# A two-block transformer on one core: which modulation rows are made where, which chunk load goes first, and how the first expert queries are formed

## The chip, the cores and the metric

One core of a Trainium2 chip runs the whole program. The metric is device time in microseconds of one execution. A core has TensorE (PE, matmuls and transposes), VectorE (DVE), ScalarE (ACT), GpSimd (POOL) and SyncE (SP); in this kernel SP only issues transfers, and POOL mostly issues gathers. Sixteen DMA engines serve the queues of all of them.

## The reference, cut to what matters

Everything is f32, with 256 tokens of 1024 columns. `x` passes the first block (two layers), then the second (two layers), in which 256 context tokens run along.

```python
for l in range(2):                                   # first block
    h = layer_norm(a*h + 0.5*swiglu(h, ffn1...))     # 2816 hidden
    h = layer_norm(a*h + mix(h @ w_in) @ w_out)      # conv, recurrence, pool
    h = layer_norm(a*h + cross_attn(h, mem, ...))
    h = layer_norm(a*h + 0.5*swiglu(h, ffn2...))
for i in range(2):                                   # second block
    mod  = silu(c)     @ ada_w[i] + ada_b[i]         # 6 x 1024 columns
    modc = silu(c_ctx) @ ada_w[i] + ada_b[i]
    h  = modulate(rms_norm(x,  gain1), sh1, sc1)     # h*(1+scale)+shift
    hc = modulate(rms_norm(xc, gain1), csh1, csc1)
    x = x + g1 * (attention(h, hc) @ w_o[i])
    if i == 0: xc = xc + cg1 * (attention(hc, hc) @ w_o[i])
    h2 = modulate(rms_norm(x, gain2), sh2, sc2)
    x = x + g2 * peer_ffn(h2)
    if i == 0: xc = xc + cg2 * peer_ffn(modulate(rms_norm(xc, gain2), ...))
```

`peer_ffn` makes 8 queries of 256 columns for each token, takes the best 16 of 128 x 128 expert keys for each, fetches for each of those 128 experts a row of `u` and a row of `v`, and adds `gate * gelu(u . h2) * v`.

## The kernel before

**Stages.** The context tokens of the second block's first layer come first (0 to about 237 us): the first modulation columns, qkv, `ctx_attention` in four units of four heads and queries, then W_o and the keys of their experts. Then the first block runs for x (to about 1763 us). Its feed forwards take the hidden columns in FT = 22 tiles: on PE `gate_up(ft)` (L1494, 32 matmuls) and `down(ft)` (L1502, 16), on DVE `hidden_tile(ft)`, which multiplies silu(gate) by up. `gate_up` runs a tile ahead, so the order at the end of one is gate_up(21), down(20), down(21). Beside it POOL gathers the experts of the context tokens (L697, 512 KB each) and DVE takes their dot products and weighted sums in `some_slots`. After the last layer_norm the second block does x: qkv, attention, W_o, `first_scores` (the first queries and keys), and then 256 gathers of pairs a layer (L738, 1 MB each) with their products, and the same for the second layer.

**The chunk ring.** Weights other than those of the feed forwards come over one SP queue in chunks of 512 KB into `wring`, four slots; `chunk_done` counts consumed chunks, and a load waits for the chunk four before it. SP works strictly in order, so a load that waits holds all behind it. `ff_loads` fill the feed forwards' own places `fw` on the same queue, three transfers a tile, two tiles ahead. `query_loads` and `kept_load` fetch query weights of the second block into places that are free by then.

**The modulation rows.** silu(c) and silu(c_ctx) times `ada_w` is made in rows of 512 output columns, each from four chunks (2 MB). 12 rows go through the ring. A row is made in one of two ways:

- on PE, `mod_row_part` (L839): two matmuls of 2 rows x 512 columns a chunk, in one of the gaps that `ctx_attention` or a layer_norm has; ACT's `mod_row_take` copies the row out and stores it
- on DVE, `mod_row_sums` (L3092 once and L3095 seven times): the chunks are scaled and added into `row_acc`, `chunk_done` gets all four counts after the last, then one PE product (L1526) sums over partitions.

Rows 0 and 1 are made by PE inside `ctx_attention`, row 2 in the context's `peer_scores`. Each of the two layers of the first block makes four: one on DVE at the end of each feed forward (before `hidden_tile(21)`, with L1526 just before `down(21)`), and one on PE in each of two layer_norms (after cross attention and after the second feed forward). `ROW_AT` says which columns a row holds. At the start of the second block all rows have been stored and are read back into `mod_tm`; PE transposes them, and DVE adds the bias into `mods` and `gains`.

**The tail of the context tokens.** `finish` (L1451) transposes their summed experts in 16 transposes, and a gated add (L2598, eight operations) puts them into `ctx_t`; both stand in `first_scores(0)` now, far from where the context tokens' second-layer keys are made.

**The first queries.** After W_o's last group, x is squared (ACT), averaged over columns by PE (L806), the root is taken on ACT, inverted on DVE (L2380), multiplied into x (L2383), and ACT `modulate` scales and shifts each of eight column groups. `first_queries` (L1218) then waits for `mod_ready(k)` for each and multiplies; ACT takes the result, `part_scores` (L1227) compares it with the keys, and DVE's `first_head` finds the indices for which POOL's first gather waits. In the second layer `own_query` (L902), the attention part left over, stands before and after them, four products each.

Of the kernel before, what the change touches and what calls it, by code (L numbers as in the profile page):

```python
# [21 lines left out]
ALU = mybir.AluOpType  # L22
# [34 lines left out]
CTX_MOD_ROWS = 3  # L57
ROW_AT = 0, 1, 2, 4, 3, 5, 6, 7, 8, 9, 10, 11
# [14 lines left out]
ROW_LOADS = (FIRST_ADA - WR + QKV_CHUNKS + WO_CHUNKS + 2 * PQ_CHUNKS) // WR + CTX_MOD_ROWS + 1  # L73

# [133 lines left out]
def program(nc, a, out):  # L208

    with ExitStack() as ctx:  # L210
# [67 lines left out]
        ada_in = sems(" ".join(f"ada_in_{s}" for s in range(GR)))  # L278
        ff_done = [gate_done, up_done, down_done]
# [74 lines left out]
        def vec(tile, where, name, i=0, n=1):  # L354
# [51 lines left out]
        pq_b = view(arena, 4096, 16, P)  # L406
        probs_b = view(arena, 4096, 2, 2 * T)
# [26 lines left out]
            ctx_t.rearrange("p k t -> p (k t)")[:, i * D:(i + 1) * D] for i in range(2)] + [  # L434
            view(arena, at, D) for at in (14848, 15872, 13824)]
# [56 lines left out]
        def _(eng):  # L492
# [55 lines left out]
            for l in range(L):  # L548
                mix_at, row_at = l * MIX_CHUNKS, CTX_MOD_ROWS + 4 * l
                for w in range(2):  # L550
# [3 lines left out]
                    if w == 0:  # L554
                        mod_row_loads(row_at)
                    else:
                        chunk_loads(a["mix_w"], mix_at + (MIX_CHUNKS - WR), WR)
                        mod_row_loads(row_at + 1)
                        mod_row_loads(row_at + 2)
                    with sp.loop(FT_TURNS, **ff_turn) as i:  # L560
                        for ft in range(FT_STEP):
                            for part in range(3):
                                ff_loads(i * FT_STEP + (l * (2 * FT) + (w * FT + 2 + ft)), ft, part)
                    if w == 0:
                        chunk_loads(a["mix_w"], mix_at, MIX_CHUNKS - WR)
                    else:
                        mod_row_loads(row_at + 3)
# [51 lines left out]
            load(0, a["second_w"][FIRST_ADA + QKV_CHUNKS + WR])  # L619
            for i, dead in enumerate(KEPT_DEAD[DEAD_EARLY:]):  # L620
                load(1 + i, a["second_w"][FIRST_ADA + QKV_CHUNKS + WR + 1 + i])
                kept_load(0, FIRST_ADA, dead)
# [122 lines left out]
        def _(eng):  # L745
# [329 lines left out]
            def block_attention():  # L1075
# [3 lines left out]
                tm_group(2, ps_b[:, 512:D], h2)  # L1079
                qk_stats(0, 4, True)  # L1080
# [47 lines left out]
            def ctx_weighted(u):  # L1128
# [7 lines left out]
                if u < 2:  # L1136
                    mod_row_free()
                else:
# [7 lines left out]
            def ctx_attention():  # L1146
# [16 lines left out]
            def first_scores(l):  # L1163

                rms(FIRST_BLOCK)
                if l == 1:
                    for k in range(4):
                        own_query(1, k, ps_a[:, 1536:2048], LAST_BLOCK)
                if l == 0:
                    finish()  # L1170
                    eng.wait_ge(mod_tm_in, 16)
                    nc.tensor.transpose(ps_d[:, 0:2 * ADA_CHUNKS], mod_tm[0:2 * ADA_CHUNKS, :],
                                        ident[0:2 * ADA_CHUNKS, 0:2 * ADA_CHUNKS]).then_inc(ada_done, pe.adds(ada_done))
                for i in range(LAST_PART):
                    for c in range(*QUERY_PARTS[i]):
                        if i:
                            early_query(l, i, c)
                        elif c == 0:
                            first_queries(l)
                        if (i, c) == (0, 1):  # L1180
                            if l == 0:
# [2354 lines left out]
```

## Time and profile before

| | us |
|---|---|
| median of three runs | 3305.03 (3302.08 to 3306.79) |
| the profiled execution | 3290.4 |
| its span | 3288.5 |
| PE busy | 3084.1 (94%) |
| DVE busy | 2111.8 (64%) |
| POOL busy | 1221.7 (37%) |
| ACT busy | 951.1 (29%) |

The mean granted clock of TensorE is 0.993. Busy time is a mean over stages that differ, so the stages have to be read by themselves. The chain of work that ended last is 65% PE, 17% DMA, 7% DVE and 5% ACT. The rows below give start and length in us; a bracket says how long the engine was idle before the row and what ended that.

### The profile page before, as it was taken

What the parts mean: (1) busy time and instruction counts of PE and PEld (TensorE: products, weight loads), DVE (VectorE), ACT (ScalarE), POOL (GpSimd) and SP (SyncE); (2) the same over time, 40 slices, a digit from 0 to 9 for tenths busy, and PEclk for the clock granted to TensorE, in tenths of its full rate; (3) what the DMA queues carried; (4) which work ended last, traced back from release to release, by engine and by line L of the source; (5) the groups of instructions that cost most, each with busy time, mean ns of one, the idle gap of its engine ahead of it and who ended that gap; (6) DMA issues with size and microseconds to landing.
All of it is one profiled execution on the core that took longest, in us unless ns stands there. A gap on an engine that the chain in (4) does not pass through costs nothing.

```text
span 3288.5 us, 39667 instructions
## 1 busy us (share of the span) xinstructions
PE 3084.1 (94%) x13217; PEld 2185.8 (66%) x13217; DVE 2111.8 (64%) x4281; ACT 951.1 (29%) x2489; POOL 1221.7 (37%) x1129
## 2 busy tenths in 40 slices
PE   8999999999999999999999999978989999997777
PEld 5598888887887888887886755533435855542224
DVE  6776787766555456765455596577565587587544
ACT  2310012121001002221002364335446464444333
POOL 1003554343444442353440144434444045454332
PEclk9999999999999999999999999999999999999999
DMA  9687988788998996788996799999999799999998
GB/s 351 215 299 287 374 339 305 267 325 338 356 347 336 365 345 231 242 326 338 370 355 241 292 421 420 420 419 404 410 422 420 293 419 421 421 421 422 421 421 356
DMA packets 252614, 1165.52 MB, mean 354 GB/s; under 512 B 27321, under 2 KB 34969, under 8 KB 186417
## 3 DMA queue, kind: packets, MB, share of 16 engines
q0 software_dynamic: 152784, 825.30, 62.3%
q1 hardware_dynamic: 99632, 338.30, 28.4%
q8 instruction: 80, 1.31, 0.2%
q14 instruction: 70, 0.57, 0.0%
q10 hardware_dynamic: 48, 0.05, 0.0%
HBM read 1162.44 MB, written 1.10 MB: 354 GB/s over the span
## 4 chain that ended last, share of the span: by engine, by line
PE 65%; DMA 17%; DVE 7%; ACT 5%; issue 2%; SPq 0%; POOL 0%; ACTq 0%; DVEq 0%; POOLq 0%
PE ps_b L1494 18%; PE ps_a L1432 13%; DMA ring<-in_peer_uv,idx 12%; PE ps_a L1502 9%; PE ps_b L776 6%; PE ps_a L763 5%; ACT arena L1721 3%; DVE ring L2883 2%; DMA arena<-in_peer_uv,idx 2%; DMA wring<-in_second_w 2%; PE ps_b L785 1%; PE ps_b L1261 1%; ACT L1721 1%; PE ps_b L1202 1%; PE ps_b L1254 1%
## 5 line engine op out<-in xcount | busy, mean ns | idle before, releaser
L1432 PE MATMUL ps_a<-ring,arena 128*128 128x512 f32 x1728 | 823.3, 611 | 131.0 <-ACT arena L1721 130.4
L738 POOL DMA_INDIRECT ring<-in_peer_uv,idx x448 | 498.4, 1112 | 888.7 <-PE ps_a L1432 624.7
L2883 DVE SCALAR_TENSOR_TENSOR ring<-ring,h_tm 128x1024 f32<-128x1024 f32 x448 | 546.6, 1222 | 381.7 <-DMA ring<-in_peer_uv,idx 381.0
L697 POOL DMA_INDIRECT ring<-in_peer_uv,idx_now x512 | 577.1, 1127 | 427.9 <-DVE arena L2711 163.8
L1432 PEld LDWEIGHTS ps_a<-ring,arena 128*128 128x128 f32 x1728 | 309.3, 192 | 564.5 <-ACT arena L1721 291.3
L1494 PE MATMUL ps_b<-x_t,ring 128*128 128x256 f32 x2816 | 623.6, 380 | 2.0 <-DMA ring<-in_ffn 1.1
L1494 PEld LDWEIGHTS ps_b<-x_t,ring 128*128 128x128 f32 x2816 | 533.0, 190 | 81.5 <-issue 3.5
L1721 ACT ACTIVATE arena<-ps_b 128x256 f32<-128x256 f32 (+3 forms) x226 | 103.6, 460 | 1254.7 <-PE ps_b L1494 829.5
L1502 PE MATMUL ps_a<-arena,ring 128*128 128x256 f32 x1408 | 318.7, 380 | 0.0
L2711 DVE SCALAR_TENSOR_TENSOR arena<-ring,h_tm 128x1024 f32<-128x1024 f32 x256 | 299.4, 1219 | 25.0 <-DMA ring<-in_peer_uv,idx_now 24.5
L1502 PEld LDWEIGHTS ps_a<-arena,ring 128*128 128x128 f32 x1408 | 267.5, 190 | 39.3 <-issue 3.5
L1721 ACT ACTIVATE wts<-dots 128x1 f32<-128x1 f32 (+1 forms) x514 | 103.7, 202 | 606.3 <-DVE ring L2883 523.6
L3064 DVE SCALAR_TENSOR_TENSOR arena<-ps_b,arena 128x256 f32<-128x256 f32 x88 | 37.3, 424 | 336.3 <-PE ps_b L1494 193.1
L1721 ACT ACTIVATE arena<-consts,wts 128x128 f32<-128x128 f32 x512 | 205.5, 401 | 66.5 <-PE ps_a L1432 20.7
L776 PE MATMUL ps_b<-x_t,wring 128*128 128x256 f32 x896 | 197.8, 381 | 6.6 <-ACT x_t L1721 6.6
L2720 DVE SCALAR_TENSOR_TENSOR arena<-ring,stage,arena 128x1024 f32<-128x1024 f32 x160 | 195.1, 1277 | 4.0 <-DMA ring<-in_peer_uv,idx_now 3.9
L776 PEld LDWEIGHTS ps_b<-x_t,wring 128*128 128x128 f32 x896 | 166.9, 190 | 34.0 <-issue 8.1
L763 PE MATMUL ps_a<-arena,wring 128*128 128x256 f32 (+1 forms) x896 | 169.1, 350 | 1.9 <-DMA wring<-in_second_w 1.0
L763 PEld LDWEIGHTS ps_a<-arena,wring 128*128 128x128 f32 x896 | 150.6, 191 | 20.1 <-issue 2.0
L1721 ACT ACTIVATE wts<-wts,gates 128x1 f32<-128x1 f32 x512 | 150.7, 294 | 16.6
L2720 DVE SCALAR_TENSOR_TENSOR arena<-ring,wts,arena 128x1024 f32<-128x1024 f32 x92 | 115.0, 1287 | 49.5 <-DMA ring<-in_peer_uv,idx_now 49.5
L1721 ACT ACT_TABLE_LOAD x107 | 137.3, 1283 | 12.0 <-PE ps_b L1494 8.7
(444 smaller groups left out, 3341.0 us busy)
## 6 DMA issues: line engine op xcount, KB each, us to landing
ring<-in_ffn SPq DMA_DIRECT2D x264, 512.0 KB, 7.1
wring<-in_second_w SPq DMA_DIRECT2D x174, 512.0 KB, 5.3
wring<-in_mix_w SPq DMA_DIRECT2D x128, 512.0 KB, 5.7
ring<-in_ada_rows POOLq DMA_DIRECT2D x36, 512.0 KB, 6.3
ring<-in_second_w SPq DMA_DIRECT2D x12, 1024.0 KB, 9.9
ring<-in_peer_uv,idx_now POOLq DMA_INDIRECT x512, 8.6
ring<-in_peer_uv,idx POOLq DMA_INDIRECT x448, 14.8
arena<-in_second_w SPq DMA_DIRECT2D x13, 512.0 KB, 8.1
```

The lines of the kernel that those rows point to most:

```text
L697: G.indirect_dma_start(rows[:, s, :], None, table, bass.IndirectOffsetOnAxis(ap=idx_now[:, half, s:s + 1], axis=0)).then_inc(rows_in[s], p ...
L738: G.indirect_dma_start(pairs[slot].rearrange("p c d -> p (c d)"), None, a["peer_uv"], bass.IndirectOffsetOnAxis(ap=idx[:, b, s:s + 1], axi ...
L763: ins = mm(acc_t[:, j, cols], w[:, k * P:(k + 1) * P], src[:, k, cols], start=k == 0, stop=k == KT - 1)
L776: ins = mm(bank[:, t * T:(t + 1) * T], w[:, k * P:(k + 1) * P], src[:, k, :], start=k == 0, stop=k == KT - 1)
L1432: ins = mm(ps_a[:, b * D + j * 512:b * D + (j + 1) * 512], diags[:, at % DIAGS, :], pairs[at % PAIRS][:, 1, j * 512:(j + 1) * 512], start= ...
L1494: ins = mm(bank[:, part * T:(part + 1) * T], fw[:, ft % 2, part, k * P:(k + 1) * P], x_t[:, k, :], start=k == 0, stop=k == KT - 1)
L1502: ins = mm(acc_t[:, j, :], fw[:, ft % 2, 2, j * P:(j + 1) * P], hidden[:, ft % 2, :], start=False, stop=last, skip_group_check=True)
L1721: return nc.scalar.activation(out, in_, func, **k)
L2711: V.scalar_tensor_tensor(acc[s % 2], rows[:, s, :], 1.0, h, ALU.mult, ALU.mult, accum_out=out).then_inc(row_used, ve.adds(row_used))
L2720: ins = V.scalar_tensor_tensor(acc[s % 2], rows[:, s, :], w, acc[s % 2], ALU.mult, ALU.add)
L2883: V.scalar_tensor_tensor(row, row, 1.0, h_tm[:, n // SLOTS, :], ALU.mult, ALU.mult, accum_out=dots[:, n % SLOTS:n % SLOTS + 1]).then_inc(d ...
L3064: V.scalar_tensor_tensor(hidden[:, ft % 2, :], ps_b[:, (ft % 2) * 512 + T:(ft % 2 + 1) * 512], 0.5, silu[:, ft % 2, :], ALU.mult, ALU.mult ...
```

## The change

Four things change.

1. **Rows.** `CTX_MOD_ROWS` goes from 3 to 1. Two rows leave `ctx_attention`, and the only one left in the context stage is made in `peer_scores`. W_o's chunks are loaded ahead of it. DVE's `ada_tiles` in `ctx_attention` come one after each `ctx_max`. The two rows go to the DVE at the head of two feed forwards: the second of layer 0 and the first of layer 1 (`HEAD_ROWS`). In these, the head row's chunks are loaded before the tile loop and its sums precede `hidden_tile(0)`; its product on PE (`row_total`) stands before gate_up(21). The chunks of the row at their end (`FF_ROWS`) are now loaded after the loop's last tile, so that SP's order at the end of the loop is the loads of tile 21, then four chunks, then the next stage's. The two other feed forwards keep their order. `row_total` also waits till the row before has been taken by ACT.
2. **Context tail.** `finish` runs on PE in the last layer_norm, ahead of the second mean; the gated add runs on DVE at the start of the second block, and PE waits for it before the key statistics of the context tokens.
3. **First queries.** In both layers `raw_queries` replaces `first_queries`: PE multiplies x times its gain, which ACT makes beside the squares, with one more column for the shift. DVE multiplies the result by 1/rms and adds the shift's part, two operations of 128 x 256. `modulate` still runs for all later queries, and `mod_ready` is waited for after `part_scores`. In the second layer own_query is divided two before and six after.
4. **SP order.** In the first layer's attention two chunks of the last query groups, FIRST_Q + 4 and + 5, are loaded ahead of the six early kept loads (512 KB each) and two behind them. The last chunk of W_o is loaded one kept load earlier.

```diff
-CTX_MOD_ROWS = 3
-ROW_AT = 0, 1, 2, 4, 3, 5, 6, 7, 8, 9, 10, 11
+CTX_MOD_ROWS = 1
+ROW_AT = 0, 4, 1, 5, 6, 2, 7, 8, 3, 9, 10, 11
+FF_ROWS, HEAD_ROWS, NORM_ROWS = ((1, 4), (7, 9)), (3, 6), ((2, 5), (8, 10))
...
+            chunk_loads(a["second_w"], FIRST_ADA + QKV_CHUNKS, WO_CHUNKS)
             mod_row_loads(0)
-            mod_row_loads(1)
-            chunk_loads(a["second_w"], FIRST_ADA + QKV_CHUNKS, WO_CHUNKS)
-            mod_row_loads(2)
...
-                    if w == 0:
-                        mod_row_loads(row_at)
+                    if w == 1:
+                        chunk_loads(a["mix_w"], mix_at + (MIX_CHUNKS - WR), WR)
+                        mod_row_loads(NORM_ROWS[l][0])
+                    if w != l:
+                        mod_row_loads(HEAD_ROWS[l])
                     else:
-                        chunk_loads(a["mix_w"], mix_at + (MIX_CHUNKS - WR), WR)
-                        mod_row_loads(row_at + 1)
-                        mod_row_loads(row_at + 2)
+                        mod_row_loads(FF_ROWS[l][w])
                     with sp.loop(FT_TURNS, **ff_turn) as i:
...
                                 ff_loads(i * FT_STEP + (l * (2 * FT) + (w * FT + 2 + ft)), ft, part)
+                    if w != l:
+                        mod_row_loads(FF_ROWS[l][w])
...
             query_loads(0, FIRST_ADA, 4, AHEAD_CHUNKS // 2)
+            chunk_loads(a["second_w"], FIRST_Q + WR, 2)
             for i in KEPT_DEAD[:DEAD_EARLY]:
                 kept_load(0, FIRST_ADA, i)
-            chunk_loads(a["second_w"], FIRST_Q + WR, WR)
+            chunk_loads(a["second_w"], FIRST_Q + WR + 2, 2, 2)
...
                 ctx_scores(0)
                 qk_stats(4, 3, False)
-                mod_row_part(0, 0, 2)
                 ctx_scores(1)
-                mod_row_part(0, 2, WR)
                 ctx_weighted(0)
                 ctx_scores(2)
-                mod_row_part(1, 0, WR)
                 ctx_weighted(1)
...
+            def row_total():
+                ...
+                eng.wait_ge(chunk_done, pe.now(chunk_done))
+                mod_row_free()
+                mm(ps_d[0:2, :], mean_d[:, 0:2], row_acc, start=True, stop=True).then_inc(
+                    row_summed, pe.adds(row_summed))
...
+                if two_rows:
+                    row_total()
                 gate_up(FT - 1)
                 down(FT - 2)
...
+                row_total()
                 down(FT - 1, True)
...
+            def raw_queries(l):
+                eng.wait_ge(query_used, ve.next(query_used, AHEAD_CHUNKS if l else 2))
+                raw = ps_b[:, 0:2 * (P + 1)].rearrange("p (c t) -> p c t", t=P + 1)
+                V.tensor_tensor(pq_b[:, 0:2, :], raw[:, :, 0:P], bcast(std[:, FIRST_BLOCK].unsqueeze(1), 2, P),
+                                ALU.mult).then_inc(dve_step, ve.adds(dve_step))
+                eng.wait_ge(dve_step, ve.now(dve_step))
+                V.tensor_tensor(pq_b[:, 0:2, :], pq_b[:, 0:2, :], bcast(raw[:, :, P:P + 1], 2, P), ALU.add).then_inc(
+                    pq_taken, ve.adds(pq_taken))
...
+                if w != l:
+                    mod_row_sums(HEAD_ROWS[l])
                 hidden_tile(0)
```

## Rows read from the trace of the kernel before

**Rows 1.** Windows: length, busy time of each engine, clock, DMA share, GB/s.
```profile
1003.00:1246.00 243.00, 240.65 (x1107) 209.12 (x1106) 130.53 (x235) 19.20 (x41) 107.65 (x99) 1.00 0.89 335
...
1763.00:1880.00 117.00, 111.72 (x579) 79.30 (x578) 57.88 (x157) 43.39 (x115) 4.77 (x5) 0.99 0.77 278
1880.00:2555.00 675.00, 608.30 (x2098) 322.12 (x2096) 449.66 (x1059) 333.12 (x959) 287.67 (x252) 0.99 1.00 413
```

**Rows 2.** Timeline of PE in the context attention.
```profile
102.10 1.89 PE L1124 MATMUL ps_a<-keys_t,arena 128*128 128x256 f32 x8
103.92 7.03 PE L839 MATMUL ps_b<-wring,cond 128*2 128x512 f32 x16
...
114.90 1.89 PE L1124 MATMUL ps_a<-keys_t,arena 128*128 128x256 f32 x8
...
124.17 1.95 PE L1142 MATMUL ps_b<-arena,vals 128*128 128x512 f32 x4 [0.83 <-ACT arena L1721]
126.86 1.32 PE L763 MATMUL ps_a<-arena,wring 128*128 128x256 f32 x5 [0.73 <-issue]
```

**Rows 3.** Timeline of DVE, then ACT, in the same stretch.
```profile
102.32 1.22 DVE L2589 TENSOR_TENSOR arena<-arena,stats 128x1024 f32<-128x1024 f32 x1
104.03 1.23 DVE L2578 TENSOR_REDUCE stats<-ps_a 128x4 f32<-128x1024 f32 x1 [0.48 <-PE ps_a L1124]
...
105.49 0.47 ACT L1721 ACTIVATE arena<-ps_a,stats 128x256 f32<-128x256 f32 x1 [2.59 <-DVE stats L2580]
```

**Rows 4.** Timeline of PE after idle time, in two places.
```profile
1825.14 3.65 PE L1011 MATMUL ps_b<-wring,arena 128*128 128x512 f32 x4 [2.67 <-DMA wring<-in_second_w]
...
1830.35 1.88 PE L1011 MATMUL ps_b<-wring,arena 128*128 128x512 f32 x4
...
2563.53 2.72 PE L879 MATMUL ps_b<-arena,wring 128*128 128x128 f32 x22 [2.50 <-ACT arena L1721]
```

**Rows 5.** Timeline of PE, then DVE, end of layer 0's second feed forward.
```profile
986.32 1.02 PE L1526 MATMUL ps_d<-arena,consts 128*2 128x512 f32 x2
987.27 3.72 PE L1502 MATMUL ps_a<-arena,ring 128*128 128x256 f32 x16
...
978.76 5.75 DVE L3095 SCALAR_TENSOR_TENSOR arena<-wring,cond,arena 128x512 f32<-128x512 f32 x7
```

**Rows 6.** Timeline of SP there.
```profile
965.84 10.69 SPq L515 DMA_DIRECT2D ring<-in_ffn  x4
984.53 2.16 SPq L498 DMA_DIRECT2D wring<-in_second_w  x4
```

**Rows 7.** DMA of 976 to 984: packets, MB, share; issues, KB each, us to landing.
```profile
DMA packets 644, 2.36 MB, mean 294 GB/s; under 512 B 69, under 2 KB 69, under 8 KB 644
...
ring<-in_ffn SPq DMA_DIRECT2D x1, 512.0 KB, 7.3
ring<-in_peer_uv,idx_now POOLq DMA_INDIRECT x4, 7.7
```

**Rows 8.** Timeline of PE, last layer_norm and start of the expert queries.
```profile
1757.74 1.99 PE L1534 MATMUL ps_d<-arena,consts 128*128 128x256 f32 x8 [1.10 <-DVE arena L3180]
...
1855.21 2.05 PE L763 MATMUL ps_a<-arena,wring 128*128 128x128 f32 x16 [0.97 <-DMA wring<-in_second_w]
1857.10 2.02 PE L806 MATMUL ps_c<-arena,consts 128*128 128x128 f32 x16
1858.96 1.91 PE L1451 MATMUL ps_a<-consts,h_tm 128*128 128x128 f32 x16
...
1861.72 3.81 PE L1218 MATMUL ps_b<-arena,ring 128*128 128x128 f32 x32 [0.76 <-ACT arena L1721]
1866.09 0.68 PE L1227 MATMUL ps_a<-subk,arena 128*128 128x128 f32 x4 [0.56 <-ACT arena L1721]
```

**Rows 9.** Timeline of DVE there, and one row of PE, second layer.
```profile
1861.97 3.22 DVE L2598 SCALAR_TENSOR_TENSOR ctx_t<-ps_a,mods,ctx_t 128x256 f32<-128x256 f32 x8
...
2608.78 0.71 PE L1227 MATMUL ps_a<-subk,arena 128*128 128x128 f32 x4 [0.47 <-ACT arena L1721]
```

More of the change, by code:

```diff
@@ L73 @@
 ROW_LOADS = (FIRST_ADA - WR + QKV_CHUNKS + WO_CHUNKS + 2 * PQ_CHUNKS) // WR + CTX_MOD_ROWS + 1
+MIX_LOADS = MIX_CHUNKS // WR
+ROW_TURNS = {row: ROW_LOADS + turns for row, turns in (
+    (1, 0), (3, MIX_LOADS + 2), (4, MIX_LOADS + 3), (6, MIX_LOADS + 5), (7, MIX_LOADS + 6), (9, 2 * MIX_LOADS + 8))}
 PAIRS = 8
@@ L406, in program @@
         pq_b = view(arena, 4096, 16, P)
+        raw_x = view(arena, 4480, KT, P + 1)
         probs_b = view(arena, 4096, 2, 2 * T)
@@ L618, in _ @@
             chunk_loads(a["second_w"], FIRST_ADA + QKV_CHUNKS, WR)
[L619 to L622, printed above, removed]
+            chunk_loads(a["second_w"], FIRST_ADA + QKV_CHUNKS + WR, WR - 1)
+            kept_load(0, FIRST_ADA, KEPT_DEAD[DEAD_EARLY])
+            load(WR - 1, a["second_w"][FIRST_ADA + QKV_CHUNKS + WO_CHUNKS - 1])
+            for i in KEPT_DEAD[DEAD_EARLY + 1:]:
+                kept_load(0, FIRST_ADA, i)
             for i in KEPT_ATTENDED:
@@ L1535, in mean_of_pairs, with layer_norm @@
                 return ins
-            def layer_norm(between, feeds=False):
+            def layer_norm(between, feeds=False, inside=None):
                 between(0, 4)
@@ L1693, in _ @@
                 layer_norm(mod_row_between, True)
-                feed_forward(h_take)
-                layer_norm(mod_row_between, l + 1 < L)
+                feed_forward(h_take, l == 0)
+                layer_norm(mod_row_between, l + 1 < L, finish if l == L - 1 else None)
             pe.skip(h_done, KT)
@@ L1977, in first_scores, with raw_rms @@
                 part_scores_take(2)
+            def raw_rms(l):
+                act(raw_x[:, :, P], mods[:, l, 24:24 + KT, 0], ACT.Copy)
+                for j in range(4):
+                    eng.wait_ge(x_added, ac.next(x_added, 2))
+                    act(sq2[:, 2 * j:2 * j + 2, FIRST_BLOCK], x_t[:, 2 * j:2 * j + 2, FIRST_BLOCK], ACT.Square).then_inc(
+                        sq2_done, ac.adds(sq2_done))
+                    for k in range(2 * j, 2 * j + 2):
+                        act(raw_x[:, k, 0:P], x_t[:, k, FIRST_BLOCK], ACT.Copy, scale=gains[:, l, 1, k, 0:1]).then_inc(
+                            raw_done, ac.adds(raw_done))
+                deviation(FIRST_BLOCK)
+                modulate(l, 1, 0, FIRST_BLOCK)
+                ac.skip(query_used, 2)
             def part_query_take(i):
@@ L3028, in _ @@
             qk_norm(3, False, 0)
-            ve.skip(chunk_done, 2 * WR)
-            ctx_over(0)
-            ctx_max(1)
-            ada_tiles(1)
-            ctx_over(1)
-            for u in range(2, 4):
-                ctx_max(u)
-                ada_tiles(4 - u)
+            for u in range(3):
                 ctx_over(u)
-            ada_tiles(1)
+                ctx_max(u + 1)
+                ada_tiles(1)
+            ctx_over(3)
+            ada_tiles(2)
             ve.skip(pt_done, 8)
@@ L3082, in later_search, with mod_row_sums @@
                     expert_ids(0, 1, 4, split=True)
-            def mod_row_sums(l, w):
-                loads = ROW_LOADS + l * (MIX_CHUNKS // WR + 4) + w * (MIX_CHUNKS // WR + 2)
+            def mod_row_sums(row):
+                if row > CTX_MOD_ROWS:
+                    eng.wait_ge(row_summed, ve.next(row_summed))
                 for k in range(KT):
@@ L3089, in mod_row_sums @@
                     if k % 2 == 0:
-                        eng.wait_ge(weights_in[k // 2], 16 * loads)
+                        eng.wait_ge(weights_in[k // 2], 16 * ROW_TURNS[row])
                     if k == 0:
```

103 lines of the change are left out of this document (51 added, 52 removed).

## The prediction

> **What bounds the kernel now.** I read the windows by stage first [rows 1]. In a feed forward PE is busy for 240.65 of 243.00 us with the DMA share at 0.89: that stage is set by PE, and anything that makes PE wait there is paid in full. In the expert stages the DMA share is 1.00 at 413 GB/s and PE has 67 us of idle time in 675: the gathers set the pace, and work of PE is free there. Between them, 1763 to 1880, PE is busy 111.72 of 117.00 and the DMA share is 0.77, so an earlier first gather means that the saturated stretch starts earlier. I then read the timelines around each edit, for whose wait ends last, and the DMA view where a load moves. The sum is made against the profiled execution, 3290.4 us, which lies 14.6 below the median of the runs shown (3305.03); I add its result to the median.
>
> **Rows out of the context attention: 6 us won (5.0 to 8.2).** A row is 7.03 us of PE, as at 103.92, and two of them stood in this stage [rows 2]. They don't come back one for one, since the units are a chain of PE, DVE and ACT. I re-timed it. Scores of unit 2 come at 102.10; the first row stands before them, but part of its time only covers the DVE and ACT work of unit 0, whose transposes, copies and values (1.2, 1.3 with the waiting, 1.95) still have to come first: of 7.03 I count 2.9 as freed, so they come near 99.2. From scores(2) to scores(3) it was 12.8 us. Without the row in it the chain is scores 1.9, reduce 1.23 and a small subtraction, four exponentials at 0.47, copies with 0.83 of waiting, values 1.95 less what overlaps [rows 2, 3]: 8.0. From scores(3) to W_o's first product it was 11.96, and 11.5 is left, because a pair of `ada_tiles` no longer stands in front. W_o's start goes from 126.86 to 118.7, 8.2 earlier. But PE now idles for some 3.5 us twice, where a row filled the time. The trace has one such place that bears on the clock: after 2.67 us of idle time four matmuls took 3.65 instead of 1.88, 1.8 us more, at half the rate [rows 4]; after 2.50 us at another place 22 matmuls took 2.72, 0.124 each against 0.128 at 1855.21 [rows 4, 8], so with no loss. Twice 1.6, a little less than that, is what I allow for the worst. I take 6, two thirds of the way to the bad end. W_o's chunks are loaded ahead of the remaining row, so they are there in time. DVE's `ada_tiles` fill its own idle time.
>
> **SP order: 5.4 us won (2.7 to 5.4).** PE waits 2.67 us for a chunk at 1825.14 and then loses 1.8 to the clock [rows 4]; that chunk stands behind the early kept loads, 3 MB, and is now in front of two thirds of what held it. 3 MB at 413 GB/s is 7.6 us, more than the wait. The stall goes, 4.4. If the clock falls anyway, 2.7. The kept loads, 1 MB more behind, are read in the expert stage, whose queries only begin after W_o; if one were late there, it would cost what 1 MB takes, 2.5. The stall of 0.97 at 1855.21 is W_o's last chunk [rows 8], which now stands one 512 KB load (1.3 us) earlier: it goes. What is next late is ACT and PE itself, nothing of the queue.
>
> **First queries: 2.3 us won (1 to 2.6).** In the first layer rms ends at 1859.1, finish takes 1.91, and L1218 starts at 1861.72 after 0.76 of waiting; the keys' product starts at 1866.09 [rows 8]. Now the raw product (eight columns more, 3.9 us) starts at 1859.1, ends at 1863.0, and DVE needs two operations of 128x256 (0.40 each, as the eight of the gated add [rows 9], so about 0.9 with the step between): part_scores at 1864.0, 2.1 earlier. The nine extra ACT operations lie beside W_o's last groups, but ACT's rms also has to come out behind them: that could eat 0.4 or, at worst, 1. The root and its inverse need ACT and DVE once each and lie beside the product. In the second layer the gain is that of the wait of 0.47 [rows 9], 0.3, because PE works through; two own_query products more now stand behind the keys, not before. I take 2.0 and 0.3. `modulate` on ACT has the raw product, part_scores and the transposed modulation rows to hide behind; if it came out late, the early queries would wait by at most what is won here.
>
> **Context tail: 0.6 us lost (0.5 to 0.8).** The 16 transposes are 1.91 us [rows 8]. In the last layer_norm PE waits 1.10 us for DVE before the second mean [rows 8], so 1.1 of them is hidden and 0.8 is not; I take 0.6, because the mean then finds its squares further on. The gated add, 3.22 us of DVE [rows 9], goes to the start of the second block, where DVE has nothing for PE; if that cover failed PE would be late by 3.22.
>
> **The row at the end of two feed forwards: 14.2 us lost (6.4 to 18.8).** This is where the sum is decided. Until now the row's chunks came before the tile loop, and DVE's sums, eight operations, 0.82 each (5.75 for seven), were done at 984.5 with PE's down(21) at 987.27 [rows 5]. Now SP issues them behind tile 21's loads, which wait in the loop: their last issue ends at 976.5 [rows 6]. From there the four chunks, 2.1 MB, share the engines with tile 21's last 0.5 MB and four gathers (x4, 7.7 us to landing, that is to about 987). In that stretch the DMA moves 294 GB/s, and a 512 KB load takes 7.3 us [rows 7]. Together 4.7 MB are to move.
>
> - At 413 GB/s [rows 1] they would be through at 987.9.
> - At 294 GB/s it is 992.5; and 992.3 comes out if nothing of the four moves till 987.2, then 5.1 us at 413.
> - I take 990: the low rate is in part for want of other work.
>
> After the last chunk two sums (1.64), then L1526 (0.95): down(21) starts at 992.6, 5.3 late. `hidden_tile(21)` stands behind the sums on DVE and is hidden by L1526. PE has nothing to do from 987.3 to 991.6, 4.3 us, more than the 2.67 after which its clock was low, so 1.8 more: 7.1. The other place (end of layer 1's first feed forward) has the same order and the same gathers: twice 7.1 is 14.2. At the lower bound it is 987.9 + 1.64 + 0.95 = 990.5, 3.2 late, with no fall of the clock: 6.4 for both. At the upper, 994.9 less 987.3 and 1.8: 9.4 each, 18.8. The next stage's loads, issued at 984.53 now, are freed at 991.7 [rows 6]: 7 us later where their reader is 5 to 7 later, so within 0.3. The head rows I cost at nothing: 6.6 us of sums on DVE (8 x 0.82) lie beside gate_up(0) and gate_up(1) on PE, before there is anything for hidden_tile(0); without that cover each would cost up to 6.6.
>
> The Trainium skill, page "DMA: Bandwidth & Descriptors", section "Queues, rings and completion order", says that each DMA engine takes its queues in turn, a packet each. By that, SP's queue and the gathers share evenly, the gathers are through with some 2 MB of SP, and the chunks come at about 991. The row gives less to SP (0.5 MB in 7.3 us), so the trace does not bear out even turns; by the page the loss would be some 16.
>
> **Sum.** 6 + 5.4 + 2.3 - 0.6 - 14.2 = -1.1: 3291.5 for the profiled execution, 3306 as a median. No change is the likeliest; a measurement of this kernel tells about 0.2% (6.6 us) from none.
>
> **The rivals.**
>
> - **The late chunks are not late.** If they land by 988, PE doesn't idle and the clock holds. For it: the low rate of [rows 7] is in part lack of demand, and the four chunks are ready in the queue. Against: a 512 KB load took 7.3 us there. Loss 6.4, sum 6 + 5.4 + 2.3 - 0.6 - 6.4 = 6.7 won, 3298; with the full 8.2, 3296. Chance 0.31.
> - **They land last of all.** One mechanism: SP's queue gets almost nothing until the gathers are through, and the chunks land at 993 or later. It decides from 993: there the loss is 2 x (993 + 1.64 + 0.95 - 987.3 + 1.8) = 20.2, sum -7.1, 3312. For it: [rows 7]. Against: the page's even turns, and 992.3 was the bound. Chance 0.13.
> - **What is won before 1880 is given back in the gathers.** If the expert stages end by something else than their start, 7.7 us of the SP and query gains go: sum -8.8, 3314. For it: share 1.00 there. Against: at 0.77 before it there is room to start earlier [rows 1], and a saturated stretch that starts earlier ends earlier. Chance 0.13.
> - **The forecast**, within 6.6 of no change: 0.43.
>
> The first makes faster 0.31, the next two make slower 0.26, and 0.43 is for the same. The range holds the forecast and most of the others: from 3296 (the full gain of the context stage and small loss) to 3314. The likeliest one's own range is 3300 to 3312.
>
> **What would show it.** W_o's first L763 at 118 to 122 in place of 126.86, with the granted clock of 95 to 119. At the ends of the two feed forwards, a wait of PE on DVE or a wring chunk of 2 to 5 us before down(21), with down(21) at half rate. No waits before L1011 and in W_o's last groups. L1227 some 2 us nearer to the rms than the 9.0 of before. The last mean 0.6 later after DVE. If the waits before down(21) are absent, the forecast is wrong on the fast side; if the layers behind them also wait, on the slow one.

## The result, and the profile after

The changed kernel takes 3309.58 us (median of 19 runs, 3305.31 to 3315.90) beside 3302.44 (19 runs, 3296.13 to 3307.58) of the kernel before on the same chip: ratio 1.0022, 95% interval 1.0016 to 1.0029. (A ratio here and below is the median time over that of the kernel before, run beside it on the same chip.) It is slower by 7 us, just over what can be told from no change. The forecast was 3306, 1.1 us lost, with no change as the likeliest.

The profiled execution took 3310.7, 20 us more than the 3290.4 of before. That is three times the difference of the medians, so the two traces can't be subtracted as they are; what lies between them is in the experiments (e0, e6, e10).

The waits of PE in the changed kernel (line, what ended the wait; us in total, times, longest):

```profile
PE ps_d L1497 <- DVE arena L3129: 13.5, 2, 6.9
...
PE ps_b L1150 <- ACT arena L1736: 5.9, 4, 3.6
...
PE ps_c L1143 <- DVE arena L2616: 5.3, 2, 3.5
...
PE ps_b L1689 <- issue: 4.0, 2, 2.0
PE ps_a L772 <- issue: 3.9, 2, 3.1
```

L1497 is `row_total`: the two late rows are the largest new wait, 13.5 us. L1143 and L1150 are the transposes and values of the context attention, where the rows had stood. The two rows of "issue" are times in which PE stood with nothing in the profile to wait for; I call them the stops. They lie in the output product of the cross attention (L1689) and the product after it (L772), where nothing was changed. Neither wait of before at L1011 or in W_o's last group is in this list at its old size; what is left there is 0.8.

The end of layer 0's second feed forward, timeline of PE, then of DVE (rows 5 before):

```profile
975.25 1.02 PE L1497 MATMUL ps_d<-arena,consts 128*2 128x512 f32 x2
976.20 7.17 PE L1511 MATMUL ps_b<-x_t,ring 128*128 128x256 f32 x32
983.21 3.62 PE L1519 MATMUL ps_a<-arena,ring 128*128 128x256 f32 x16
993.44 1.86 PE L1497 MATMUL ps_d<-arena,consts 128*2 128x512 f32 x2 [6.61 <-DVE arena L3129]
995.23 4.99 PE L1519 MATMUL ps_a<-arena,ring 128*128 128x256 f32 x16
...
985.13 0.49 DVE L3126 TENSOR_SCALAR arena<-wring,cond 128x512 f32<-128x512 f32 x1 [7.54 <-DMA wring<-in_second_w]
985.65 0.75 DVE L3129 SCALAR_TENSOR_TENSOR arena<-wring,cond,arena 128x512 f32<-128x512 f32 x1
987.62 1.54 DVE L3129 SCALAR_TENSOR_TENSOR arena<-wring,cond,arena 128x512 f32<-128x512 f32 x2 [1.22 <-DMA wring<-in_second_w]
990.14 3.25 DVE L3129 SCALAR_TENSOR_TENSOR arena<-wring,cond,arena 128x512 f32<-128x512 f32 x4 [0.97 <-DMA wring<-in_second_w]
```

DVE's brackets show the queue. The first chunk of the late row ends a wait of 7.54, the next ones 1.22 and 0.97 after the sums of the chunk before, and the fourth comes while the third is summed. The sums end at 993.4, and PE, ready since 986.8, has waited 6.61 us. Then it is slow: the product takes 1.86 in place of 1.02, near half the rate, and down(21), which gets the full rate back on the way, 4.99 in place of 3.72 [rows 5]. The other end is a copy of this one: 6.88 us of wait, 1.86 and 5.10.

The context attention, timeline of PE, first one row of the kernel before and then the changed one [rows 2]:

```profile
86.14 1.89 PE L1124 MATMUL ps_a<-keys_t,arena 128*128 128x256 f32 x8
...
85.15 1.89 PE L1134 MATMUL ps_a<-keys_t,arena 128*128 128x256 f32 x8
...
88.77 1.97 PE L1134 MATMUL ps_a<-keys_t,arena 128*128 128x256 f32 x8 [0.87 <-ACT arena L1736]
94.21 1.11 PE L1143 MATMUL ps_c<-consts,arena 128*128 128x128 f32 x4 [3.48 <-DVE arena L2616]
...
96.86 3.59 PE L1150 MATMUL ps_b<-arena,vals 128*128 128x512 f32 x4 [0.69 <-ACT arena L1736]
100.29 1.89 PE L1134 MATMUL ps_a<-keys_t,arena 128*128 128x256 f32 x8
...
106.64 3.51 PE L1150 MATMUL ps_b<-arena,vals 128*128 128x512 f32 x4 [3.59 <-ACT arena L1736]
109.94 2.11 PE L1134 MATMUL ps_a<-keys_t,arena 128*128 128x256 f32 x8
...
122.12 3.26 PE L772 MATMUL ps_a<-arena,wring 128*128 128x256 f32 x14 [0.73 <-issue]
```

The two idle times are 3.48 and 3.59, and behind each the values take 3.5 us where they took 1.96. W_o starts at 122.12; it was 126.86. Of these 4.7 us the stage itself, from scores(0) to W_o, won 3.7 (36.97 in place of 40.72); the rest is that scores(0) came 1.0 earlier.

The last layer_norm and the first expert queries, timeline of PE, then two rows of DVE [rows 8]:

```profile
1785.64 1.89 PE L1547 MATMUL ps_d<-arena,consts 128*128 128x256 f32 x8
...
1879.56 2.03 PE L815 MATMUL ps_c<-arena,consts 128*128 128x128 f32 x16
1881.42 3.74 PE L1224 MATMUL ps_b<-arena,ring 128*128 128x129 f32 x32
1884.99 0.25 PE L1179 MATMUL ps_d<-consts,mem_t 96*128 96x96 f32 x1
1886.13 0.71 PE L1234 MATMUL ps_a<-subk,arena 128*128 128x128 f32 x4 [0.89 <-DVE arena L2861]
...
1885.19 0.42 DVE L2858 TENSOR_TENSOR arena<-ps_b,std 128x256 f32<-128x256 f32 x1 [0.69 <-PE ps_b L1224]
1885.65 0.42 DVE L2861 TENSOR_TENSOR arena<-arena,ps_b 128x256 f32<-128x256 f32 x1
```

From the mean square (L815) to the keys' product it is 6.57 us, where it was 8.99: 2.4 won. (e2 and e9 have 6.57 too, e10 has 7.43.) The raw product follows the mean without a gap, and DVE's two operations are 0.42 each. From the last mean to L815 it is 93.92 where it was 99.36, 5.4 less. How much of it is the order of the SP queue, e7 tells.

### The profile page after: what moved, and what is told of

The parts are those of the page before. It is cut to its first block, busy times and chain, and to the rows that moved or that the text cites. A ratio compares the mean times of both kernels' runs of the same rounds, so it can differ in the third digit from the quotient of the medians.

```text
span 3308.8 us, 39663 instructions
## 1 busy us (share of the span) xinstructions
PE 3080.1 (93%) x13179; PEld 2189.7 (66%) x13189; DVE 2125.2 (64%) x4301; ACT 954.5 (29%) x2505; POOL 1223.5 (37%) x1129
## 4 chain that ended last, share of the span: by engine, by line
PE 64%; DMA 18%; DVE 7%; ACT 4%; issue 2%; POOL 0%; SPq 0%; DVEq 0%; ACTq 0%; POOLq 0%
PE ps_b L1511 17%; DMA ring<-in_peer_uv,idx 13%; PE ps_a L1439 12%; PE ps_a L1519 9%; PE ps_b L785 5%; PE ps_a L772 5%; ACT arena L1736 2%; DVE ring L2920 2%; DMA arena<-in_peer_uv,idx 2%; DMA wring<-in_second_w 2%; PE ps_b L1268 1%; PE ps_b L794 1%; PE ps_b L1261 1%; PE ps_b L1206 1%; ACT L1736 1%
## 5 line engine op out<-in xcount | busy, mean ns | idle before, releaser
L772 PE MATMUL ps_a<-arena,wring 128*128 128x256 f32 (+1 forms) x896 | 172.2, 354 | 6.0 <-issue 3.9
L772 PEld LDWEIGHTS ps_a<-arena,wring 128*128 128x128 f32 x896 | 152.9, 193 | 25.3 <-issue 7.7
```

The lines of the kernel that those rows point to most:

```text
L772: ins = mm(acc_t[:, j, cols], w[:, k * P:(k + 1) * P], src[:, k, cols], start=k == 0, stop=k == KT - 1)
```

## The experiments

e0, e1, e2 and e3 ran on one chip (chip 0), e4 to e7 on another (chip 1), e8 to e10 on a third (chip 9) and e11 on a fourth (chip 12). The kernel before took 3286.67, 3301.64, 3303.56 and 3287.86 there. So ratios are compared between them, not times. Each expectation stands ahead of its result.

**e0. The kernel before once more.** No edit.

> The kernel before once more, for a second profile of it. The first profiled execution took 3290.4 against a median of 3302.4. If the stops that the profile gives to 'issue' (PE in the cross attention, 2.0 us each and 3.1 before W_o's product) differ from execution to execution, this profile shows some in the same kernel and a span of about 3300. If they come from the changed program, it shows none and a span of about 3290. Time: ratio 1.0000 within 0.0007 in both.

Ratio 1.0005 (0.9995 to 1.0014), median 3287.87 beside 3286.67, profiled execution 3283.8, and no stops. So the kernel before has no stops here either, and this didn't decide whose they are; e6 and e10 do. A second use of this profile: at L1011, where 2.67 us of idle time were followed by 3.65 for four matmuls [rows 4], it shows

```profile
1820.17 1.95 PE L1011 MATMUL ps_b<-wring,arena 128*128 128x512 f32 x4 [1.70 <-DMA wring<-in_second_w]
```

1.70 of wait and no half rate. The price of that stall in the kernel before is 1.7 to 4.4, by execution. From the last mean to L806 it is 96.72 us here and was 99.36.

**e3. The rows alone.** The kernel before with part 1 of the change: the row constants, SP's row loads, `row_total`, the head sums, the context attention, and nothing of `finish`, `raw_queries` and FIRST_Q.

> The kernel before with the modulation rows moved and nothing else of the change. Theory A (the context attention wins 5 to 6, the two late rows lose 18): 12 to 13 slower, ratio 1.0038. Theory B (the rows' part is neutral and the loss is elsewhere): ratio 1.000 to 1.001.

Ratio 1.0049 (1.0036 to 1.0062), 16 us. Against e0's profile, also without stops: the first feed forward starts 4.5 us earlier, the mean behind layer 0's second one comes at 994.23 in place of 989.24, and it came 5.0 earlier before that feed forward, so 10.0 are lost in it; in the next one 9.8; from there to the end nothing changes (the spans are 16.0 apart). Of the 4.5, 3.7 are won between scores(0) and W_o. Theory A; its 18 was a little small. The first of the two ends, timeline of PE:

```profile
984.79 1.87 PE L1490 MATMUL ps_d<-arena,consts 128*2 128x512 f32 x2 [5.66 <-DVE arena L3097]
986.59 5.90 PE L1512 MATMUL ps_a<-arena,ring 128*128 128x256 f32 x16
```

**e2 and e10. All but the rows.** The kernel before with parts 2, 3 and 4. e10 is the same kernel again.

> The kernel before with all parts of the change but the modulation rows: finish in the last layer_norm, raw first queries, the order of the SP queue. Theory A (the three parts win what the working gives, 5.4 + 2.3 - 0.6 = 7.1): ratio 0.9978, 3295. Theory B (what is won before the gathers is given back in them): within 2 us of the kernel before, ratio 0.9994 to 1.0006.

> The kernel e2 once more, beside e9 on the same chip. By the sum of e2's trace (6.2 us less than the kernel before between the last layer_norm and the second layer's queries) the ratio is 0.998; by its first measurement 0.9989.

Ratios 0.9989 (0.9980 to 0.9997) and 0.9981 (0.9972 to 0.9990). Against e0's profile, e2's is 0.4 later at the last mean, 3.7 ahead at the mean square before the expert queries (so 4.1 are won in this stretch), 6.1 ahead at the keys' product, 5.2 ahead at the second layer's first mean square (2546.89 and 2552.13) and 6.2 ahead at the end: of what is won before the first layer's gathers, 0.9 at most is given back in them. (The 4.1 need not be the order's alone; e7 has the order by itself.) The two ratios make it 3.6 and 6.3 us; the first lies between the two theories, the second is Theory A's.

**e7. The SP order alone.**

```diff
             query_loads(0, FIRST_ADA, 4, AHEAD_CHUNKS // 2)
+            chunk_loads(a["second_w"], FIRST_Q + WR, 2)
             for i in KEPT_DEAD[:DEAD_EARLY]:
                 kept_load(0, FIRST_ADA, i)
-            chunk_loads(a["second_w"], FIRST_Q + WR, WR)
+            chunk_loads(a["second_w"], FIRST_Q + WR + 2, 2, 2)
```

> The kernel before with the SP order of the block attention alone: two chunks ahead of the early kept loads, W_o's last chunk one load earlier. Theory A (the waits for a chunk before L1011 and in W_o's last group end, and what the clock lost behind the first): 3 to 5 us earlier at the start of the expert gathers, ratio 0.9985 to 0.999. Theory B (in the kernel with the three parts the waits went because the transposes in front had gone, not by the order): less than 1 us, ratio 1.000.

Ratio 0.9991 (0.9982 to 1.0001), 3 us by the middle, which time alone doesn't tell from nothing. The waits of PE between the last layer_norm and the gathers:

```profile
PE ps_a L765 <- DMA wring<-in_second_w: 0.8, 1, 0.8
...
PE ps_b L1013 <- DMA wring<-in_second_w: 0.7, 1, 0.7
```

The wait before `first_query` (L1013) shrinks to 0.7 by the order alone; the one in W_o's last group stays, 0.8, and goes in e2's profile but comes back as 1.9 in e10's. So the order nearly ends the first stall, and the second depends on the execution. From the last mean to L808, the mean square, it is 95.32 us, where e0 has 96.72, the first profile of before 99.36, e2 92.62, e10 95.59 and the changed kernel 93.92 and, in e6, 94.01. The order alone is thus seen to win 1.4 to 4.0, by which profile of before it is held against, and the rest of the 5.4 is not shown to be its work.

**e1. The late row's chunks in the loop, all four.** The changed kernel, but:

```diff
+                    turns = (FT_TURNS // 2, FT_TURNS - FT_TURNS // 2) if w != l else (FT_TURNS,)
+                    for n, first_turn in zip(turns, (0, FT_TURNS // 2)):
+                        if first_turn:
+                            mod_row_loads(FF_ROWS[l][w])
+                        with sp.loop(n, **ff_turn) as i:
...
-                    if w != l:
-                        mod_row_loads(FF_ROWS[l][w])
```

> The changed kernel, but in the two feed forwards with two rows the second row's four chunks are loaded in the middle of the tile loop, five turns before its end, in place of behind it. Theory A (the late chunks cost about 9 us at each of the two ends: the waits of 6.9 us before L1526 and down(21) at half rate): both waits go, the kernel gains 15 to 18 us on the changed one and is 7 to 11 us faster than the kernel before, ratio 0.997 to 0.998. Theory B (the first block is late for another reason, the stops of PE in the cross attention that the profile gives to 'issue'): the waits before L1526 go, but the time stays within 5 us of the changed one, ratio 1.001 to 1.002.

The loop has five turns of four tiles, so the chunks stand behind the second of them, three turns before the end, not five as the expectation has it. Ratio 1.0032 (1.0021 to 1.0043): Theory A missed. The time is within 5 us of the changed kernel's, as Theory B says, but not for its reason: this profile has no stops. The waits at `row_total` are gone, and there is a new one:

```profile
PE ps_b L1514 <- DMA ring<-in_ffn: 14.1, 4, 6.6
```

```profile
858.08 8.71 PE L1514 MATMUL ps_b<-x_t,ring 128*128 128x256 f32 x32 [6.64 <-DMA ring<-in_ffn]
```

Two megabytes in front of a tile's loads make the tile 6.64 us late, and the clock falls as well, 8.71 in place of 7.07. The other of the two feed forwards has the same, 6.51 and 9.21. From their first tile to the mean behind them they take 241.9 and 241.4 us; the changed kernel has 242.4 and 241.6, the kernel before 232.3 and 232.2. The chunks weren't only in a bad place at the end.

**e4. The same chunks one by one.** The changed kernel with one chunk behind each of the first four turns.

```diff
+                    turns = [FT_TURNS // (WR + 1)] * (WR + 1) if w != l else [FT_TURNS]
+                    for q, n in enumerate(turns):
+                        with sp.loop(n, **ff_turn) as i:
...
+                        if w != l and q < WR:
+                            load(q, a["second_w"][LAYER_1 + WR * ROW_AT[FF_ROWS[l][w]] + q])
```

> The changed kernel, but in the two feed forwards with two rows the second row's four chunks are loaded one after each of the first four turns of the tile loop (a turn is four tiles, 41 us). With all four together, after the second turn (the kernel e1), tile loads came late and PE waited 14 us for them. Theory A (the fault is a burst: 2 MB in front of a tile load that has 10 us, with the DMA engines at 0.9): a single chunk takes 1.3 to 2.6 us of the queue and costs nothing, neither wait is left, and the time is 10 us under the kernel before, ratio 0.9968. Theory B (these feed forwards have no room for 2 MB more at any place): PE waits 2 to 3 us for a tile load after each chunk, four times in each, ratio 1.001 to 1.003 as in e1.

Ratio 1.0000 (0.9991 to 1.0009): half of the way between both. The waits:

```profile
PE ps_b L1515 <- DMA ring<-in_ffn: 8.4, 8, 2.3
```

Six of the eight waits, 7.6 us, lie in the two feed forwards with the extra chunks, three in each, of 0.3 to 2.3; that is 0.95 for each of the eight chunks on average. (The other two, 0.3 and 0.5, lie in other feed forwards; the changed kernel has three of such waits, 1.3 in all.) With the second product in each (0.95) the two feed forwards, 237.1 and 237.4 us long, lose 10 us in place of 20. Even one chunk between two tiles' loads was not free here, although the DMA share is 0.89 [rows 1]. So Theory B is right about the room and A about the burst.

**e5. As e4, with products in the context attention's idle times.**

```diff
+                def warm():
+                    for _ in range(10):
+                        mm(ps_b[:, u * 512:u * 512 + T], ident, ctx_t[:, 0, :], start=True, stop=True)
+                if u == 0:
+                    warm()
                 eng.wait_ge(s_prob, pe.next(s_prob))
...
+                if u == 1:
+                    warm()
                 eng.wait_ge(pt_taken, pe.next(pt_taken, 2))
```

> As e4, and PE gets ten products of 128x256 more in each of the two places where it idles in the context attention (before the transposes of unit 0 and before the values of unit 1), whose results nothing reads. Theory A (4.7 us were won there in place of 8.2 because the clock falls after 3.5 us without work: values 3.59 in place of 1.96, transposes 1.1 in place of 0.6): those rows come back to 1.96 and 0.6 and W_o's first product starts 3 to 4 us earlier than in e4, at 118 to 119. Theory B (the chain of DVE and ACT sets the pace): W_o starts at 122 as in e4 or later. In time: 3 us of 3300, hardly more than can be measured; the trace decides.

Ratio 0.9990 (0.9979 to 1.0001). The rows (the ten products stand as x20, 4.48 us):

```profile
86.85 1.89 PE L1138 MATMUL ps_a<-keys_t,arena 128*128 128x256 f32 x8
...
90.47 1.96 PE L1138 MATMUL ps_a<-keys_t,arena 128*128 128x256 f32 x8 [0.87 <-ACT arena L1748]
92.27 4.48 PE L1147 MATMUL ps_b<-ctx_t,consts 128*128 128x256 f32 x20
...
98.36 1.98 PE L1162 MATMUL ps_b<-arena,vals 128*128 128x512 f32 x4 [0.74 <-ACT arena L1748]
```

The values take 1.98 again. From scores(1) to W_o it is 30.3 us (90.47 to 120.78) where the changed kernel has 33.35 (88.77 to 122.12): the clock's part is 3.0. W_o starts 3.4 earlier than in e4's profile (124.16), but at 120.78 and not at 118 to 119, because scores(0) starts at 86.85 here. From scores(0) to W_o it is 33.93, 6.8 less than in the kernel before; the 8.2 that I had re-timed are not reached even at the full rate. Theory A.

**e6. The changed kernel again.** No edit.

> The changed kernel once more, for a second profile. Its first profile had stops of PE given to 'issue' in both cross attentions, 5.6 and 6.2 us in sum with what followed, which none of four other kernels of this case shows. If they belong to the program they are there again. If they belong to that one execution, this profile has none, and from the context attention to the start of the gathers it lies 12 us less behind the kernel before than the first one. Time: ratio 1.002 to 1.003.

Ratio 1.0025 (1.0016 to 1.0034), 3310.72 beside 3301.64. The stops are there again. They would seem to belong to the program, but for e10: the kernel of e2 shows none in one profile and these in the other:

```profile
PE ps_b L1683 <- issue: 4.0, 2, 2.0
PE ps_a L767 <- issue: 2.4, 2, 1.7
```

e2's profiled span is 3275.7 and e10's 3297.6. e7, which has only a few SP instructions in other places, has them too (4.1 and 3.8), so they don't need the change. What goes with them is the chip: none of the five profiles on chips 0 and 12 (e0 to e3, e11) has one in the cross attention, and all seven on chips 1 and 9 have at least one there. On chip 9 they differ by execution, too: e10 has both of 2.0, e8 one, and e9 none of these but one of 1.5 before W_o's product, with a profiled execution of 3286.6 beside a median of 3299.45. The first profile of the kernel before is without them, at 3290.4, while its median is 3302.4.

**e8 and e11. The changed kernel with products where it idles.** `warm` as in e5, and before the late row's product:

```diff
                 gate_up(FT - 1)
                 down(FT - 2)
+                if two_rows:
+                    mod_row_free()
+                    for _ in range(22):     # e11: 14
+                        mm(ps_d[:, 0:T], ident, x_t[:, 0, :], start=True, stop=True)
                 row_total()
```

> The changed kernel with products that nothing reads where PE idles: ten of 128x256 in each of the two places of the context attention as in e5, and 22 of 128x256 before the late row's product at the end of the two feed forwards with two rows. The loads and the waits for them stay as they are. Theory A (of the 10 us lost at each of the two ends 2.1 are the clock, L1497 1.86 in place of 1.02 and down(21) 4.99 in place of 3.72, and 7 the wait): the wait for the row stays in place under the products, down(21) takes 3.7 again, each end loses 8 in place of 10, and with 3 in the context attention the kernel is 7 us faster than the changed one, ratio 1.000 to 1.001. Theory B (the clock is no part of the loss): as the changed kernel, 1.0022.

Ratio 1.0024 (1.0014 to 1.0033), no gain. The clock did hold, but I had put a product at half of its 0.44 us, and PE came 3.1 us behind the sums:

```profile
988.06 9.66 PE L1552 MATMUL ps_d<-x_t,consts 128*128 128x256 f32 x44
997.65 1.02 PE L1505 MATMUL ps_d<-arena,consts 128*2 128x512 f32 x2
998.60 3.72 PE L1527 MATMUL ps_a<-arena,ring 128*128 128x256 f32 x16
```

> As e8, but 14 products before the late row's product in place of 22: in e8 they took 9.66 us (0.44 each) and PE came 3.1 us behind the end of the sums, so that what the clock gave back was lost again. Fourteen take 6.1. Theory A (the clock is 2.1 us of each end): down(21) at 3.7, the end of both feed forwards 2 us earlier than in the changed kernel, and with 3 from the context attention 7 us in all, ratio 1.000 to 1.001. Theory B (the clock's part is less, or it falls in the half microsecond that is left): 1.001 to 1.0022.

Ratio 1.0009 (1.0000 to 1.0018), 4 us better than the changed kernel by the medians, each against the kernel before on its own chip; the intervals overlap a little. The late row's chunks are waited for as before:

```profile
977.91 6.21 PE L1552 MATMUL ps_d<-x_t,consts 128*128 128x256 f32 x28
984.05 1.02 PE L1505 MATMUL ps_d<-arena,consts 128*2 128x512 f32 x2
985.00 3.72 PE L1527 MATMUL ps_a<-arena,ring 128*128 128x256 f32 x16
```

From down(20)'s end to down(21)'s end it is 10.8 us (977.91 to 988.65), where the changed kernel has 13.3 (986.8 to 1000.15). Of the difference of 2.6 the rows give 2.1 to the clock (the product 1.02 for 1.86, down(21) 3.72 for 4.99); the other 0.5 is that the row was summed sooner after down(20), so that the products bridge 6.1 us where PE had waited 6.6. The rest of the loss is the wait. Theory A.

**e9. The kernel e2 with products at two older stalls.** Twenty of 128x128 before the first qkv product of the context tokens, eighteen before the first level of the recurrence.

> The kernel e2 (the three parts without the rows) with products that nothing reads in two kinds of place where the kernel before idles and is slow afterwards: 20 of 128x128 before the first qkv product of the context tokens (10.10 us in place of 7.07 in e2's profile) and 18 of 128x128 before the first level of the recurrence in each layer (2.5 to 3.5 us of idle time, 3.78 in place of 1.95 in one profile). Theory A: 3 us at the first and up to 1.8 at each of the others, so 3 to 5 us faster than e2, ratio to the kernel before 0.9972 to 0.998. Theory B (the clock falls there anyway or the products come late): as e2, 0.998 to 0.999.

Ratio 0.9992 (0.9983 to 1.0001), no better than e10 (0.9981) on the same chip. The qkv group does take 7.07 in place of 10.10, but it starts at 40.38 in place of 38.61:

```profile
35.81 4.73 PE L1476 MATMUL ps_b<-consts 128*128 128x128 f32 x40
40.38 7.07 PE L780 MATMUL ps_b<-arena,wring 128*128 128x256 f32 x32
```

The products took 4.73 where PE had 2.7 to wait, which eats 1.8 of the 3.0 gained. Theory B in time; the same error of size as in e8.

The version with the lowest ratios is e2/e10: the change without its rows.

## Why the prediction came out as it did

The range held the time, but the sum was off by 6 us: 1.1 lost was forecast, 7.1 was measured (95% interval 5.3 to 9.6). The 3306 looks closer to 3309.58 than that, because it stands on a median of three runs, 3305.03, that came out 2.6 us above the 3302.44 of all nineteen; that is luck. By its steps, in us won:

| step | forecast | shown | by |
|---|---|---|---|
| rows out of the context attention | 6.0 | 3.7 | scores(0) to W_o, after against before; the same in e3 against e0 |
| SP order | 5.4 | 5.4 or 4.1, with the other parts; alone 1.4 to 4.0 | after against before; e2 against e0; e7 |
| first queries | 2.3 | 2.4 and some 0.5 | after against before |
| context tail | -0.6 | -0.6 | after |
| two late rows | -14.2 | -19.8 | e3 against e0 |
| sum | -1.1 | -7.1 in the medians, -8.4 to -9.7 in the parts | |

The parts come from single executions, which differ by more than what the two sums differ by.

**The late rows** were the right mechanism and the term that was mis-sized, 9.9 each in place of 7.1. Two things were short. The chunks came later: the sums end 17.4 us after the first of the four issues (976.03 to 993.4), and I had 15.1 (976.5 to 991.6); PE waits 6.6 and 6.9 where I had 4.3. And the clock costs 2.1 here and 3.0 in e3, whose down(21) takes 5.90, not 1.8. The head row's own product before gate_up(21), 0.95 on PE's path at 975.25, is not a third: it is named nowhere in the working, but 4.3 of idle time, 0.95 and 1.8 make 7.1, because what the product takes is taken off the wait. By the same count the changed kernel has 6.6 + 0.95 + 2.1 = 9.7. The lower bound, 3.2 each, was not approached: the shortest of the six waits of this kind in the changed kernel and e3 is 5.66.

The even turns of the Trainium skill ("DMA: Bandwidth & Descriptors", "Queues, rings and completion order") gave 991 and a loss of 16. The trace agrees with even turns while both queues had work: from 984 to 988 the changed kernel's SP queue (q1) moved 0.84 MB and the gathers' queue (q0) 0.85:

```profile
q0 software_dynamic: 230, 0.85, 51.8%
q1 hardware_dynamic: 229, 0.84, 51.0%
```

The prediction had set this rule aside for one row, the 512 KB load that took 7.3 us [rows 7]. The third chunk ends a wait of DVE at 990.14 and the fourth is there by 991.8: nearer to that rule than to the 990 that I took.

**The context attention** won 3.7, outside the 5.0 to 8.2. Two things were wrong. The re-timing itself was 1.4 too good: at the full rate the stage wins 6.8 (40.72 less e5's 33.93). And the clock took 3.0, near the worst case of 3.2, of which I had counted two thirds; e5 gives it back. PE's two idle times were longer than the 2.67 for which [rows 4] show a fall, and the kernel before had a nearer row, which the prediction does not use:

```profile
518.81 3.78 PE L1608 MATMUL ps_a<-arena 128*128 128x128 f32 x16 [3.51 <-DVE stats L3281]
```

After 3.51 us of idle time sixteen matmuls took 3.78, where they take 2.05 after 1.02 (at 1282.39): the whole 1.7.

**SP order** came out at 5.4 against the profile of before that was shown, and that agreement is in part luck. The second profile of the same kernel has 1.70 of wait and no fall, and the order alone (e7) leaves a wait of 0.7 there and one of 0.8 in W_o's last group, which was to go. The lower bound of 2.7 is above the 1.4 that e7 shows against e0.

**First queries** were right in the first layer, 2.4. In the second, the keys' product comes 2.1 earlier and the two own_query products behind it take 1.6 of that: 0.5.

**Rivals.** "The late chunks are not late" fell at once: 6.6 and 6.9 of wait. "They land last of all" is the nearest in size, and its sum of -7.1 is the measured one, but not by its mechanism: SP's queue did not stand till the gathers were through, and the chunks came by 991.8 and not 993; that the 19.8 is near its 20.2 comes in part from a larger price of the clock. "Given back in the gathers" fell: e2 is 6.1 ahead before them and 5.2 behind them, and 6.2 at the end.

What the prediction had no step for: whether two feed forwards have room for 2 MB at all. e1 and e4 say that they don't, at the places of the loop that I tried: at best 5 us for each row, against the 7 of PE time that it took in the context attention and of which only 1.9 were worth anything to the end. I took a DMA share of 0.89 to leave room.

## What to carry to other kernels

When a load is moved behind others on an in-order queue, time each of its parts and the work behind it, and add what the engine loses after it has idled for 3 us and more: here 1.5 to 3.0 us a stall, a third to a half of the wait itself. The feed forwards here, at a mean DMA share of 0.89, had no room for a burst: each extra 512 KB cost PE 1 us on average even when they came 41 us apart. Work that fills another engine's waits (the rows in the context attention) can be nearly free where it is, and moving it off a busy engine is only worth what the chain behind it shortens.

## What the runs showed of the hardware

The same program has executions up to 22 us apart: the spans of e2 and e10, one kernel on two chips, are 3275.7 and 3297.6. On one chip it can be nearly as much (e9: 3286.57 to 3306.44). The kernel before has medians of about 3287 on two of the chips and 3302 to 3304 on the two others. One place where the traces differ is the cross attention: on the slower chips PE stops for 2.0 us in its output product and up to 3.1 before the product after it, with nothing that the profile shows to wait for. Behind the first stop 16 matmuls took 2.77 in e10 in place of 1.95, and 2.05 in the changed kernel's first layer. From e2 to e10 the layer-0 cross attention's last scores come 2.3 us later and W_o's product behind it 7.1 (715.40 and 722.53). What PE stops for was not tested. The DMA load does not tell: the share is 0.98 in e10 around the stops (710 to 724) and 0.98 in e2 at the same place without them (708 to 722). The stops fit with the first profile of before, which has none, lying 12 us under its median, and with two profiles of the two kernels differing by 20 where the medians differ by 7; that they are the whole of it is not shown.

A fall of PE's granted clock shows in the next group. Behind 3.48, 3.51, 3.59, 6.61 and 6.88 us without work the next group ran at or near half rate. Behind 1.70 and 2.50 it did not, behind 2.67 it did. The length of the wait alone does not decide it, since it fell in e10 behind 1.93:

```profile
1864.98 2.80 PE L767 MATMUL ps_a<-arena,wring 128*128 128x128 f32 x16 [1.93 <-DMA wring<-in_second_w]
```

The same sixteen took 2.05 behind 0.97 [rows 8]. Filling the idle time with products kept the full rate in the groups shown (e5, e8, e9, e11), and the size of those products decided whether anything was won (e8 against e11).
